# Probabilities of the differential heads and forgetting pairs: turned by VectorE and device memory instead of TensorE, value products later

## The reference, cut to what matters

```python
# differential attention: 4 heads, each with two maps (m = 0, 1), causal
probs = softmax(where(kp <= qp, (q @ k.T) * scale, -inf))          # per head, map
weights = probs[:, :, 0] - lam * probs[:, :, 1]
o = weights @ v                                                    # then RMS norm over 128 columns
# forgetting attention: 4 heads, causal, cum = running sum of log_sigmoid(f_logit + b)
logits = (q @ k.T) * scale + cum[q] - cum[k]
o = softmax(where(kp <= qp, logits, -inf)) @ v
```

## Time and profile before

| | before |
|---|---|
| median of 3 runs | 846.55 us (846.4 to 847.26) |
| the profiled execution, its own time | 846.53 us |
| its span | 844.7 us |
| TensorE matmul busy | 840.3 us (99%), 4110 instructions |
| VectorE busy | 609.8 us (72%) |
| ScalarE busy | 445.1 us (53%) |
| GpSimd busy | 113.5 us (13%) |
| moved by DMA | 172.5 MB, mean 204 GB/s |

### The profile page before, as it was taken

The page is one execution under the profiler, slowest core; times in us unless marked ns, Lnnn a source line. Parts: engine busy times, 40 slices in busy tenths (PEclk is TensorE's granted clock), DMA queues, the critical chain, the costliest instruction groups (busy, mean ns, idle before and its releaser), DMA issues.

```text
span 844.7 us, 11101 instructions
## 1 busy us (share of the span) xinstructions
PE 840.3 (99%) x4110; PEld 697.4 (83%) x4110; DVE 609.8 (72%) x894; ACT 445.1 (53%) x650; POOL 113.5 (13%) x89
## 2 busy tenths in 40 slices
PE   9999999999999999999999999999999999999998
PEld 7878888888888888888888888888888888888887
DVE  7896978778677766665479768869697776666643
ACT  6657655754454454444375585557543644444431
POOL 0650201004501000000005402010064000000000
PEclk9999999999999999999999999999999999999999
DMA  9857666586567766666666485765765577766661
GB/s 337 286 170 227 200 211 203 164 271 191 181 200 246 208 211 202 203 221 215 195 182 175 132 242 170 241 208 150 273 188 165 172 236 209 210 196 222 219 192 50
DMA packets 102374, 172.53 MB, mean 204 GB/s; under 512 B 13104, under 2 KB 27952, under 8 KB 102320
## 3 DMA queue, kind: packets, MB, share of 16 engines
q1 hardware_dynamic: 101888, 171.16, 64.7%
q10 hardware_dynamic: 432, 0.66, 0.2%
HBM read 161.82 MB, written 4.19 MB: 197 GB/s over the span
## 4 chain that ended last, share of the span: by engine, by line
PE 93%; DVE 2%; DMA 2%; SPq 1%; ACT 1%; issue 0%; ACTq 0%
PE bulk L1774 29%; PE bulk L1778 29%; PE bulk L1775 29%; DMA raw<-in_w_in_dram 2%; DVE w_lo L1096 2%; PE bankAB L1539 1%; PE bankT L1686 0%; PE bankAB L1675 0%; PE bankAB L1633 0%; ACT w_hi L817 0%; PE bankAB L1548 0%; PE bankO L1644 0%; PE bankO L1704 0%; PE bankO L1698 0%; PE bankO L1697 0%
## 5 line engine op out<-in xcount | busy, mean ns | idle before, releaser
L1096 DVE TENSOR_TENSOR w_lo<-raw,w_hi 128x1024 fp32r<-128x1024 f32 (+1 forms) x288 | 362.2, 1276 | 113.0 <-ACT w_hi L817 110.8
L817 ACT ACTIVATE w_hi<-raw 128x1024 fp32r<-128x1024 f32 (+1 forms) x286 | 294.8, 1046 | 200.5 <-PE bulk L1778 195.2
L1774 PE MATMUL bulk<-w_hi,hT_hi 128*128 128x512 f32 (+1 forms) x880 | 342.9, 390 | 0.2 <-DVE wide L1199 0.2
L1775 PE MATMUL bulk<-w_lo,hT_hi 128*128 128x512 f32 (+1 forms) x880 | 339.2, 386 | 0.0
L1778 PE MATMUL bulk<-w_hi,hT_lo 128*128 128x512 f32 (+1 forms) x880 | 336.2, 386 | 0.0
L1774 PEld LDWEIGHTS bulk<-w_hi,hT_hi 128*128 128x128 f32 x880 | 165.3, 188 | 33.6 <-issue 0.9
L1778 PEld LDWEIGHTS bulk<-w_hi,hT_lo 128*128 128x128 f32 x880 | 165.0, 188 | 33.2
L1775 PEld LDWEIGHTS bulk<-w_lo,hT_hi 128*128 128x128 f32 x880 | 165.4, 188 | 32.0
L1774 PE MATMUL bulk<-w_hi,aT_hi 128*128 128x512 f32 x174 | 67.8, 390 | 0.0
L1778 PE MATMUL bulk<-w_hi,aT_lo 128*128 128x512 f32 x174 | 67.7, 389 | 0.0
L1775 PE MATMUL bulk<-w_lo,aT_hi 128*128 128x512 f32 x174 | 67.7, 389 | 0.0
(11 more groups left out here) (234 smaller groups left out, 712.6 us busy)
## 6 DMA issues: line engine op xcount, KB each, us to landing
raw<-in_w_in_dram SPq DMA_DIRECT2D x110, 512.0 KB, 4.4
raw<-in_w_ffn_up_dram SPq DMA_DIRECT2D x80, 512.0 KB, 4.3
raw<-in_w_ffn_down_dram SPq DMA_DIRECT2D x44, 512.0 KB, 3.7
raw<-in_w_branch_dram SPq DMA_DIRECT2D x20, 512.0 KB, 4.5
raw<-in_w_out_dram SPq DMA_DIRECT2D x16, 512.0 KB, 3.3
wide<-wide SPq DMA_DIRECT2D x160, 32.0 KB, 2.7
bias<-in_b_gate_dram SPq DMA_DIRECT2D x16, 256.0 KB, 4.7
raw<-in_w_ffn_up_dram SPq DMA_DIRECT2D x16, 256.0 KB, 3.1
```

The costliest lines, as they stand in the source:

```text
L817: act.activation(w_hi[:, g % RING, :, 0:width], raw[:, g % RAW, :, 0:width], ACT.Copy).then_inc(hi_ready, 1)
L1096: vec.tensor_tensor(w_lo[:, g % RING, :, 0:width], raw[:, g % RAW, :, 0:width], w_hi[:, g % RING, :, 0:width].bitcast(F32), ALU.subtract). ...
L1774: pe.matmul(dst, hi, whi, start=(k == ks[0]), stop=False)
L1775: pe.matmul(dst, hi, wlo, start=False, stop=False)
```

## The change

The transposes of probabilities (`tr_probs`) leave TensorE. In their place VectorE turns 32x32 blocks (`probs_turn`, right behind its part of the softmax), SyncE writes them out by one transfer and reads them back by four (`probs_to_dram`, `probs_from_dram`, at the units in `PROBS_AT`), and for a head ScalarE copies them to `probsT`, which now has one half for even and one for odd heads; for a pair TensorE reads the landed words directly as the moving operand. The products of values move: head 0 from unit 30 to 35, head 1 from 37 to 42, heads 2 and 3 from 42 to 47, pair 0 from 47 to 50; pair 1 stays at 56. VectorE's and ScalarE's lists follow, with `diff_norm` and the turn of `diff` from slot 48 to 49, behind the softmax and turn of pair 1, and the rows of `diff` by device memory from slots 52 and 53 to 53 and 54. In scores and probabilities the smaller part (queries 0 to 127) now stands in columns 0 to 127 and the larger in 128 to 383, so that the three blocks stand in the order in which the product wants them. GpSimd's squares of `o_d` go to another scratch area (TA for TB).

```diff
 MIXING_PE = [
     (9, "tr_ss"), (14, "sb_scores", 0), (18, "sb_sums", 0), (20, "sb_out", 0), (20, "sb_scores", 1), (23, "sb_sums", 1),
-    (24, "tr_qk", "dk"), (25, "sb_out", 1), (25, "scores", "diff", 0), (30, "tr_probs", "diff", 0), (30, "scores", "diff", 1),
-    (30, "pv", "diff", 0), (35, "cum"), (35, "scores", "diff", 2), (35, "tr_probs", "diff", 1), (37, "scores", "diff", 3),
-    (37, "pv", "diff", 1), (37, "tr_forget"), (39, "tr_probs", "diff", 2), (42, "pv", "diff", 2), (42, "tr_probs", "diff", 3),
-    (42, "scores", "fox", 0), (42, "pv", "diff", 3), (47, "tr_probs", "fox", 0), (47, "scores", "fox", 1), (47, "pool_a"),
-    (47, "pv", "fox", 0), (50, "pool_b"), (52, "tr_probs", "fox", 1), (56, "pv", "fox", 1), (68, "tr_merged", 0),
-    (73, "tr_merged", 1)]
+    (24, "tr_qk", "dk"), (25, "sb_out", 1), (25, "scores", "diff", 0), (30, "scores", "diff", 1), (35, "cum"),
+    (35, "scores", "diff", 2), (35, "pv", "diff", 0), (37, "scores", "diff", 3), (37, "tr_forget"), (42, "pv", "diff", 1),
+    (42, "scores", "fox", 0), (47, "pv", "diff", 2), (47, "scores", "fox", 1), (47, "pool_a"), (47, "pv", "diff", 3),
+    (50, "pool_b"), (50, "pv", "fox", 0), (56, "pv", "fox", 1), (68, "tr_merged", 0), (73, "tr_merged", 1)]
 
 _PE = [(0, "tr_norm", "attn", 0, 1)] + MIXING_PE + [(F0, "tr_norm", "ffn", 0, 1)]
...
-BY_DRAM = ('dq', 'fox', 'diff')
-for _s in ('fox', 'diff'):
-    for _a, _way in enumerate(("out", "back")):
-        SPREAD_AT.setdefault(TURN_AT[_s] + AHEAD + _a, []).append((_s, _way))
-for _s in ('dq',):
-    SPREAD_AT.setdefault(TURN_AT[_s] + AHEAD, []).extend([(_s, "out"), (_s, "back")])
+ROWS_AT = {"dq": (20, 20), "fox": (37, 38), "diff": (53, 54)}
+BY_DRAM = tuple(ROWS_AT)
+PROBS_AT = {("diff", 0): (31, 33), ("diff", 1): (36, 39), ("diff", 2): (41, 43), ("diff", 3): (43, 45), ("fox", 0): (45, 47),
+            ("fox", 1): (52, 55)}
+for _s, _at in ROWS_AT.items():
+    for _u, _way in zip(_at, ("out", "back")):
+        SPREAD_AT.setdefault(_u, []).append((_s, _way))
+for _s, _at in PROBS_AT.items():
+    for _u, _way in zip(_at, ("probs_out", "probs_back")):
+        SPREAD_AT.setdefault(_u, []).append((_s, _way))
 for _p, _u in enumerate(FF_TURN):
...
+    (27, "softmax", "diff", 0), (30, "pf"), (30, "fox_forget"), (32, "softmax", "diff", 1), (34, "probs_evac", "diff", 0),
+    (36, "softmax", "diff", 2), (37, "forget_evac"), (38, "softmax", "diff", 3), (39, "fox_evac", "fq"),
+    (39, "fox_evac", "fk"), (41, "probs_evac", "diff", 1), (42, "softmax", "fox", 0), (46, "probs_evac", "diff", 2),
+    (46, "probs_evac", "diff", 3), (46, "sigmoid", 0, 0), (48, "softmax", "fox", 1), (48, "pool_evac_a"),
+    (48, "sigmoid", 0, 1), (48, "sigmoid", 1, 0), (48, "sigmoid", 1, 1), (49, "pool_evac_b"), (50, "pv_evac", "fox", 0),
+    (53, "sigmoid", 2, 1), (53, "sigmoid", 2, 0), (55, "diff_evac", 1), (55, "diff_evac", 0), (56, "pv_evac", "fox", 1),
+    (60, "sigmoid", 3, 0), (61, "sigmoid", 3, 1), (69, "merged_evac", 0), (72, "merged_evac", 1)]
...
+    (25, "maxima", "diff", 0), (27, "softmax", "diff", 0), (27, "probs_turn", "diff", 0), (29, "pf"), (29, "fox_norm"),
+    (29, "fox_forget"), (30, "maxima", "diff", 1), (32, "softmax", "diff", 1), (32, "probs_turn", "diff", 1), (32, "gate", 0),
+    (32, "cum_evac"), (33, "maxima", "diff", 2), (33, "turn", "fox"), (36, "pv_evac", "diff", 0), (36, "gate", 1),
+    (37, "softmax", "diff", 2), (37, "probs_turn", "diff", 2), (37, "maxima", "diff", 3), (39, "softmax", "diff", 3),
+    (39, "probs_turn", "diff", 3), (39, "fox_evac", "fq"), (39, "fox_evac", "fk"), (40, "gate", 2), (41, "pv_evac", "diff", 1),
+    (41, "maxima", "fox", 0), (41, "softmax", "fox", 0), (41, "probs_turn", "fox", 0), (44, "gate", 3),
+    (47, "pv_evac", "diff", 2), (47, "maxima", "fox", 1), (47, "pv_evac", "diff", 3), (48, "softmax", "fox", 1),
+    (48, "probs_turn", "fox", 1), (49, "diff_norm"), (49, "turn", "diff"), (49, "gate", 4), (49, "pool_evac_b"),
+    (51, "pv_evac", "fox", 0), (52, "gate", 5), (55, "diff_evac", 1), (55, "diff_evac", 0), (56, "gate", 6),
+    (57, "pv_evac", "fox", 1), (60, "gate", 7), (69, "merged_evac", 0), (71, "merged_evac", 1)]
...
+        probs_turning = {"diff": wide[:, 0, 3072:3456], "fox": wide[:, 0, 3072:3840]}
+        probs_spread = {**{("diff", h): wide[:, h % 2, 2048:2432] for h in range(4)},
+                        ("fox", 0): wide[:, 1, 3072:3840], ("fox", 1): probs_room[:, 384:1152]}
...
+        def probs_to_dram(engine, layer, job):
+
+            if layer:
+                wait_probs(engine, layer - 1, job)
+            engine.wait_ge(probs_turned, nth(probs_turned, layer, job))
+            engine.dma_start(dram_probs[job].rearrange("a r b x -> (a r) b x"),
+                             probs_turning[job[0]].rearrange("p (b x) -> p b x", b=NQUAD)).then_inc(probs_out, 16)
+
+        def probs_from_dram(engine, layer, job):
+
+            if job in (("diff", 2), ("diff", 3)):
+                engine.wait_ge(probsT_ready, nth(probsT_ready, layer, job[1] - 2))
+            if job == ("fox", 1):
+                engine.wait_ge(stage_done, nth(stage_done, layer, ("pv", "diff", 3)))
+            engine.wait_ge(probs_out, 16 * nth(probs_out, layer, job))
+            for b in range(NQUAD):
+                engine.dma_start(probs_spread[job][b * QUAD:(b + 1) * QUAD, :].rearrange("p (a x) -> p a x", a=NQUAD),
+                                 dram_probs[job][:, :, b, :].rearrange("a r x -> r a x")).then_inc(probs_back, 16)
...
-                act.wait_ge(stage_done, nth(stage_done, layer, ("tr_probs", kind, h)))
-                ins = act.activation(probsT[:, 0, :], bank["T"][:, 0:384], ACT.Copy)
-                if kind == "fox":
-                    ins = act.activation(probsT[:, 1, :], bank["O"][:, 0:384], ACT.Copy)
-                ins.then_inc(probsT_ready, 1)
+
+                wait_probs(act, layer, (kind, h))
+                if layer or h >= 2:
+                    act.wait_ge(stage_done, nth(stage_done, layer, ("pv", "diff", h - 2)) if h >= 2 else
+                                nth(stage_done, layer - 1, ("pv", "fox", 1)))
+                act.activation(probsT[:, h % 2, :].rearrange("p (k g q) -> p k g q", k=3, g=NQUAD), probs_blocks((kind, h))[:, 0, :, :, :],
+                               ACT.Copy).then_inc(probsT_ready, 1)
...
+                if g == 6:
+
+                    vec.wait_ge(probs_out, 16 * nth(probs_out, layer, ("fox", 1)))
...
+            def probs_turn(layer, kind, h):
+
+                vec.wait_ge(probs_ready, nth(probs_ready, layer, (kind, h)))
+                before = jobs[jobs.index((kind, h)) - 1]
+                if layer or (kind, h) != jobs[0]:
+                    at = layer if (kind, h) != jobs[0] else layer - 1
+                    vec.wait_ge(probs_out, 16 * nth(probs_out, at, before))
+                n = len(probs_of[kind])
+                turned = probs_turning[kind].rearrange("p (g i k q) -> p i k g q", g=NQUAD, i=n, k=3)
+                for i in range(n):
+                    last = vec.transpose(turned[:, i, :, :, :], probs_of[kind][i].rearrange("p (k g q) -> p k g q", g=NQUAD, q=QUAD))
+                last.then_inc(probs_turned, 1)
...
-                pe.wait_ge(probsT_ready, nth(probsT_ready, layer, (kind, h)))
                 if kind == "diff":
+                    pe.wait_ge(probsT_ready, nth(probsT_ready, layer, h))
                     pe.wait_ge(v_ready, nth(v_ready, layer, ("dv", 1)))
                     take("O", o_d_ready, layer, h)
                     v = [v_d[:, t, h * P:(h + 1) * P] for t in range(TT)]
                     o = bank["O"]
-                    pe.matmul(o[:, 0:P], probsT[:, 0, 0:P], v[0], start=True, stop=False, skip_group_check=True)
-                    pe.matmul(o[:, P:SEQ], probsT[:, 0, P:SEQ], v[0], start=False, stop=False, skip_group_check=True)
-                    ins = pe.matmul(o[:, P:SEQ], probsT[:, 0, SEQ:SEQ + P], v[1], start=False, stop=True, skip_group_check=True)
+                    pe.matmul(o[:, 0:P], probsT[:, h % 2, 0:P], v[0], start=True, stop=False, skip_group_check=True)
+                    pe.matmul(o[:, P:SEQ], probsT[:, h % 2, P:SEQ], v[0], start=False, stop=False, skip_group_check=True)
+                    ins = pe.matmul(o[:, P:SEQ], probsT[:, h % 2, SEQ:SEQ + P], v[1], start=False, stop=True, skip_group_check=True)
                 else:
+                    wait_probs(pe, layer, (kind, h))
+                    blocks = probs_blocks((kind, h))
                     pe.wait_ge(v_ready, nth(v_ready, layer, ("fv", 1)))
                     take("O", lhs_lo, layer, ("fox", h))
                     halves = [(bank["O"][i * HD:(i + 1) * HD, :], slice((2 * h + i) * HD, (2 * h + i + 1) * HD)) for i in range(2)]
                     for i, (o, v) in enumerate(halves):
-                        pe.matmul(o[:, 0:SEQ], v_f[:, 0, v], probsT[:, i, 0:SEQ], start=True, stop=False, skip_group_check=True)
```

(31 more changed lines are left out.)

61 lines of the change are left out of this document (30 added, 31 removed).

## The result

The changed kernel took 871.01 us (median, 870.63 to 872.95), the kernel before 846.9 us on the same chip (846.4 to 847.26): ratio 1.029, 95% interval 1.0274 to 1.0307. That is 24.1 us slower, where 12.6 were forecast, and 1 us above the range. The direction was right, and so were the wait for pair 1 and the clock behind it; one wait was put in the wrong place and priced far too low.

A forecast was written before the change was run, and what follows sets the result against it. TensorE's matmul time was taken to bound the kernel. Per layer, -2.5 saved + waits 0.3 + 1.7 + 0.2 + 4.7 + clock 1.9 = +6.3 us; two layers +12.6 on 846.5 gave 859.1 us, range 846 to 870.

The forecast's parts named there:

- Removed from TensorE: 24 probability transposes a layer leave TensorE: net 2.5 us a layer saved, 5.0 in all (4.4 to 5.6).
- Added to VectorE: VectorE's four single and four paired transposes a layer, 8 x 0.5 = 4 us, mostly fitting into idle time.
- First place: TensorE waits at unit 45 for VectorE's split, delayed by turns and head 2's write: 0.3 us a layer (0 to 1.2).
- Second place: Head 3's product in unit 47 waits for bank O, freed by `pv_evac` of head 2: 1.7 us a layer (0 to 3.5).
- Third place: Unit 53: `diff_norm` and turn stand behind unit 52's split, VectorE's 3.1 us lead goes: wait 0.2 us (0 to 0.7).
- Fourth place: Pair 1's product in unit 56 waits for reads behind the differential rows in SyncE's list: 4.7 us a layer (1.3 to 7.5).
- The clock: After the wait at unit 56 TensorE runs 3.9 us at half speed, losing 1.9 us a layer (0 to 3.9).
- That the clock would hold: Rival: the long wait at unit 56 comes but the clock stays at full: 855.3 us, chance 0.20.
- The signs of being wrong: TensorE idle under 1 us; differential rows' read back under 4 us after write's issue; unit 53's split 3 us ahead.
- Short landings: Rival: write lands in 3.2 us, pieces in 2.6, so unit 56 waits 1.3 and clock holds: 848.5 us, chance 0.12.
- The overload rival: Rival: 60 more transfers crowd the queues and delay weight loads too: above 870 us, chance 0.05.

The follow-up runs named there:

- two places: Changed kernel with two buffers used in turn for a head's turned probabilities, so head h's turn waits for head h - 2's write: 859.6 us, ratio 1.0156.
- earlier write: Changed kernel with head 2's write moved in SyncE's list from slot 41 to slot 39, ahead of head 1's reads back: 859.06 us, ratio 1.0149.
- both edits: Changed kernel with two alternating buffers for a head's turned probabilities and pair 1 read back at unit 53 instead of 55: 843.21 us, ratio 0.9965.
- gate 4 first: As both edits, plus gate 4 ahead of `diff_norm` in VectorE's list at unit 49: 842.71 us, ratio 0.9954, beside 843.59 us without it.
- the matmuls that fill: Changed kernel plus matmuls nobody reads, 36 ahead of pair 0's scores (unit 42) and 80 ahead of pair 1's product (unit 56): 865.47 us, ratio 1.0231.
- the traffic alone: Kernel before plus the change's transfers with a constant as source, TA for TB, gates 4 and 6 waiting for the last ones: 846.64 us, ratio 1.0001.

## Why the prediction was wrong

By its own steps, layer 0 and layer 1 of the trace after:

- **Removed from TensorE, 2.5 a layer:** right. Up to unit 41 TensorE was 1.83 us ahead; all stages without a wait sum to 2.5 and 2.3. With both waits gone, 3.2 us are gained, about 1 is left in the bank O wait and 0.7 in unit 51's stage: some 5, as forecast.
- **Added to VectorE, 128x384 taken as 0.54 us:** 0.58 for a head, 1.04 for a pair (twice 128x384); no wait of TensorE came from these durations as such.
- **First place, unit 45, 0.3 us:** this is the step that failed, by place and by size. The prediction named the turn that waits for head 2's write, priced it at "0.5 to 2" without working it out from SyncE's list, as it had done for pair 1, and carried it only to the split of unit 45. Nearer behind that turn stands `fox_evac`, whose keys TensorE wants at unit 42, three units earlier. VectorE waited 4.0 and 5.9 us, TensorE 2.3 and 4.1, where 0.3 a layer was forecast, and its stage grew by 3.3 and 5.2. The three experiments on this step (two places, earlier write, both edits) put it at 11.4 to 12.0 us with the clock behind it.
- **Second place, bank O, 1.7:** the mechanism is right, but only once TensorE is on time: none in the kernel after, up to 0.5 a layer in the version with both edits (0.9 once with gate 4 first), 1.1 with the matmuls that fill. Two waits in a row don't add where TensorE's first gives VectorE the time to be ready at the second.
- **Third place, unit 53, 0.2:** no wait, but the lead fell from 3.1 us to 0.75, and to 0.4 in the version with both edits; the arithmetic held to some tenths.
- **Fourth place, pair 1, 4.7:** right in mechanism, and the other term that was too small: the stage grew by 5.7 and 7.4, of which 5.0 and 6.7 idle and the rest the product itself at the lower clock. With t = 173.5 in layer 0, the write was issued at t + 0.5 (0.45 forecast), the reads began 5.15 behind it (5.1), pair 1's at t + 7.9 (7.7) and TensorE was there at t + 9.1 (8.4), and it started at t + 14.1 (13.1). The last of the four pieces was issued 1.4 us behind the first (1.3), and they landed after 3.8 to 4.7 (4.1).
- **The clock, 1.9 a layer in one stretch:** there were two. In the units behind the waits they cost 2.2 and 1.3 us in layer 0, 2.1 and 2.0 in layer 1; with the scores and the product that ran at the lower level too, 3.2 and 1.9, and 3.2 and 2.7. So 1.9 was right for pair 1 in layer 0 and low elsewhere, and the missing stretch followed from the missed wait. The rows of the warm-up from which the 1.9 came show a granted clock of 1.00 throughout; its 3.9 us at half speed were read from the spacing of the matmuls, and no run here tests that. That the clock would hold (a chance of 0.20) was wrong at both places.
- **The signs of being wrong:** none of the three that the prediction named came (TensorE was idle, the rows' read back began 5.15 us behind their write, unit 53's split was 0.75 ahead). They watch the places that it had thought of, and the failed step lay beside them.
- **Short landings (0.12):** not so. The rows' write took 5.15 us (6.4 in layer 1) and the pieces 3.8 and more, not 3.2 and 2.6. The estimate beside it by the Trainium skill, page "DMA: Bandwidth & Descriptors", section "Anatomy of one DMA", 3.2 and 2.2, was as low or lower; that section is on transfers that GpSimd issues, and these are SyncE's.
- **The overload rival, above 870 us (0.05):** the time was there and the mechanism was not, as the traffic alone shows.

So 12.6 forecast and 24.1 measured differ, over both layers, by the idle time of the first place (6.5 instead of 0.6), that of the fourth (11.7 instead of 9.4) and the clock (about 11 instead of 3.8, of which 6.4 behind the first place), less the second and third (3.8 forecast, none), and 0.2 less saved: 5.9 + 2.3 + 7.2 - 3.8 + 0.2 = 11.8, by the span's 24.4. So it was luck that the forecast missed by no more: two forecast waits that didn't come took 3.8 us off an error of 15.4.

## What to carry to other kernels

When a result goes by device memory, two lists decide: follow every wait in the issuing engine's list (what stands between "ready" and "issued"), and every wait for a buffer in the computing engine's list down to the first consumer behind it that TensorE wants, not to the one you have in mind. A wait for a landing cost twice on TensorE here, once idle and once at the lower clock. A second place for a buffer, or the swap of two entries in a queue, can be worth more than the change it serves: here the two turned 2.9% slower into 0.4% faster.

## What the runs showed of the hardware

- The same 192 KB write from SBUF took 2.0 to 8.0 us to land (median 4.0, eight writes); what set it is not shown. The Trainium skill, page "DMA: Bandwidth & Descriptors", section "Anatomy of one DMA", which is on transfers that GpSimd issues, gives a fixed part of about 2.0 us and the bytes at 436 GB/s; an estimate by it for this write is 2.45 us. The trace agrees for the quickest only: SyncE's writes landed after 2.0, 2.4 and six times 3.9 to 8.0.
- An idle time of TensorE of 2.33 us was followed by the lower clock for the next 6 us, at 0.50 with TensorE busy throughout; behind one of 5.00 us the clock had fallen before the idle time ended (0.50 from 185.0 to 187.7). With the matmuls that fill, waits of 0.8 to 2.0 us left it at 1.00 in the profiled execution.
- 60 more transfers, 6.3 MB written and read in all, changed the time by 0.01% (-0.08 to +0.1%).
